# Second products of two MLPs and a gated network as seven accumulated block products

## The reference

```python
# twice, D_FF = 4096
h = rms_norm(x, ln_mlp_pre[l])
x = x + rms_norm(jnp.square(jax.nn.relu(h @ mlp_w1[l])) @ mlp_w2[l], ln_mlp_post[l])
# once, D_FF_2 = 2816
x = x + (jax.nn.silu(h @ w1) * (h @ w3)) @ w2
```

## Time and profile before

| | us |
|---|---|
| median of 3 runs | 2972.57 |
| lowest and highest | 2966.53, 2977.65 |
| the profiled execution | 2970.6 |
| its span, first to last instruction | 2968.8 |
| mean granted TensorE clock | 0.986 of full |
| first MLP, from hT's second half to the last second product | 539.46 to 744.11 |
| second MLP | 1259.31 to 1464.0 |
| gated network | 1609.1 to 1830.1 |

### The profile page before, as it was taken

One profiled execution on the slowest core, in us unless ns is written; L12 is line 12 of the kernel. 1 busy time (PEld: TensorE's weight loads), 2 busy tenths in 40 slices (PEclk: granted clock), 3 DMA queues, 4 the chain that ended last, 5 costly groups with the idle time before them and its releaser, 6 DMA issues.

```text
span 2968.8 us, 37497 instructions
## 1 busy us (share of the span) xinstructions
PE 2845.2 (96%) x16514; PEld 2101.4 (71%) x16514; DVE 824.2 (28%) x1461; ACT 336.2 (11%) x687; POOL 91.0 (3%) x130
## 2 busy tenths in 40 slices
PE   7999998999999999899999999989999999999998
PEld 6689775676678867577676777557776776776775
DVE  2554112434255311233444453230001001001001
ACT  1220211000222111100032000210000000000000
POOL 0011200000001110000000000000000000000000
PEclk9999999999999999999999999989999999999999
DMA  5231342444333243244342433339999999999995
GB/s 228 92 142 72 135 154 80 163 170 171 107 135 114 74 154 141 100 156 163 131 154 114 164 134 120 136 125 381 378 362 362 385 352 363 386 356 370 372 386 233
DMA packets 59193, 617.18 MB, mean 208 GB/s; under 512 B 6800, under 2 KB 7056, under 8 KB 8976
## 3 DMA queue, kind: packets, MB, share of 16 engines
q1 hardware_dynamic: 56880, 603.27, 52.8%
q0 software_dynamic: 2144, 11.45, 1.0%
HBM read 613.64 MB, written 1.05 MB: 207 GB/s over the span
## 4 chain that ended last, share of the span: by engine, by line
PE 88%; DVE 5%; DMA 4%; ACT 1%; issue 1%; SPq 0%; DVEq 0%; ACTq 0%
PE ps L680 14%; PE ps L1403 14%; PE ps L1119 8%; PE ps L1126 8%; PE ps L1010 8%; PE ps L1413 7%; PE ps L1423 6%; PE ps L990 4%; PE ps L1443 3%; PE ps L1022 2%; PE ps L661 2%; PE ps L721 2%; DMA slabA<-in_ev_ffn_w 1%; PE ps L1101 1%; PE ps L1284 1%
## 5 line engine op out<-in xcount | busy, mean ns | idle before, releaser
L1403 PEld LDWEIGHTS ps<-work,slabA 128*128 128x128 f32 x3584 | 406.0, 192 | 45.2 <-issue 45.2
L1403 PE MATMUL ps<-work,slabA 128*128 128x128 f32 x3584 | 416.7, 277 | 0.9 <-issue 0.9
L1126 PE MATMUL ps<-slabB,work 128*128 128x512 f32 x688 | 301.9, 592 | 0.0
L1010 PE MATMUL ps<-hT,slabA 128*128 128x256 f32 x1024 | 232.3, 380 | 1.1 <-ACT work L1635 1.1
L1126 PEld LDWEIGHTS ps<-slabB,work 128*128 128x128 f32 x688 | 127.7, 190 | 145.4 <-issue 145.4
L680 PE MATMUL ps<-hT,slabA 128*128 128x256 f32 x992 | 219.5, 381 | 1.3 <-DMA slabA<-in_ev_w_in 0.7
L1010 PEld LDWEIGHTS ps<-hT,slabA 128*128 128x128 f32 x1024 | 192.2, 190 | 28.3 <-ACT work L1635 1.9
L680 PEld LDWEIGHTS ps<-hT,slabA 128*128 128x128 f32 x992 | 187.9, 191 | 28.0 <-issue 1.4
L1413 PE MATMUL ps<-fbT,work 128*64 128x256 f32 x1792 | 205.7, 382 | 1.8 <-DMA fbT<-in_od_exp_w 1.8
L1423 PE MATMUL ps<-slabB,work 128*128 128x512 f32 x448 | 202.0, 593 | 0.0
L1413 PEld LDWEIGHTS ps<-fbT,work 128*64 128x64 f32 x1792 | 123.6, 137 | 85.5 <-issue 26.3
(11 more groups left out here) (373 smaller groups left out, 2757.3 us busy)
## 6 DMA issues: line engine op xcount, KB each, us to landing
slabA<-in_od_exp_w SPq DMA_DIRECT2D x56, 2048.0 KB, 9.6
fbT<-in_od_exp_w SPq DMA_DIRECT2D x56, 2048.0 KB, 9.9
slabB<-in_od_exp_w SPq DMA_DIRECT2D x56, 1024.0 KB, 8.4
fbT<-in_od_exp_w SPq DMA_DIRECT2D x56, 1024.0 KB, 10.7
slabA<-in_w_in SPq DMA_DIRECT2D x24, 2048.0 KB, 7.8
slabA<-in_mlp_w SPq DMA_DIRECT2D x32, 1024.0 KB, 6.8
slabB<-in_mlp_w SPq DMA_DIRECT2D x32, 1024.0 KB, 4.8
slabA<-in_ev_ffn_w SPq DMA_DIRECT2D x11, 2048.0 KB, 10.6
```

Of the source, the lines that this page charges most:

```text
L1010: last = mm(ps[:, b, 0:T], side["gates"][:, k, c % 4 * P:(c % 4 + 1) * P], hT[:, k, :], start=(k == 0), stop=(k == KD - 1))
L1126: last = mm(ps[:, 4 + 2 * t + half, :], he[:, j, t * P:(t + 1) * P], w2[:, j, half * 512:(half + 1) * 512], start=(i == 0 and j == 0), sto ...
L1403: last = mm(ps[:, 0, (2 * w + j) * P:(2 * w + j + 1) * P], v[:, k, j * P:(j + 1) * P], xs[:, k, :], start=(k == 0), stop=(k == KD - 1))
```

## The change

The second product of a step is also made as seven block products, of 128 hidden columns x 128 tokens with 512 columns each. Each of the seven has a PSUM bank of its own, 1 to 7, in which it accumulates over all steps but the last two; then they are combined once, in PSUM (`first_tokens`, `second_tokens`), and the last two steps are added to the result in the old form. For this VectorE forms four sums of slabB (`down_sums_of`) and four of the hidden block (`hidden_sums_of`) in each step. The block products of the first product have only bank 0 left: they are made in groups of four and three, ScalarE copies each group to SBUF, and the next group waits for that copy. TensorE therefore takes groups of the first product and parts of the second in turn. `combine` reads the copies and needs one operation less. The weight sums have two buffers instead of three, and three semaphores of other stages (`fox_ln`, `gla_cum`, `gla_exps`) are replaced by ones that exist already, with the same order.

The new parts and the loops, cut (the code that they replace is printed above; `up_sums` forms the sums of slabA as `sums` did, `gate_of` and `hidden` call `combine` and add the Silu's product or the square, `plain` is a plain step; in the gated network the stage begins with the token sums, `up_sums(1, 0)`, `plain(0)`, `down_sums_of(0)`, `hidden_sums_of(0)`, `up_sums(1, 1)`):

```diff
+        def up_bank(i, w, part, steps):
+            return 2 * w + part if i == steps - 1 else 0
...
-                ringA.load(sp, [((lambda s: s[:, 0:w13.shape[1]]), w13)], ("hidden_psum", 2) if i < plain_steps(gated) else ("up_products", 1 + gated))
+                ringA.load(sp, [((lambda s: s[:, 0:w13.shape[1]]), w13)], ("hidden_psum", 2) if i < plain_steps(gated) else ("up_products", 2 * (1 + gated)))
...
+                    factors = ((a11, b11), (a12, b21), (sa[:, 0], sb_[:, 0]), (sa[:, 1], sb_[:, 1]), (sa[:, 2], sb_[:, 2]), (sa[:, 3], b22), (a22, sb_[:, 3]))
+                    bank = up_bank(i, w, part, steps)
+                    if bank > 1:
+                        pe.wait_ge(sem("sums_ready"), due("pe", "sums_ready"))
+                    elif (i, w, part) != (begun, 0, 0):
+                        pe.wait_ge(sem("products_out"), due("pe", "products_out"))
+                    for c, (lhs, rhs) in enumerate(factors[4 * part:4 * part + 4]):
+                        if c == 2 and part == 0:
+                            pe.wait_ge(sem("sums_ready"), due("pe", "sums_ready"))
+                        for k in range(4):
+                            last = mm(ps[:, bank, c * P:(c + 1) * P], lhs[:, k, :], rhs[:, k, :], start=(k == 0), stop=(k == 3))
+                    last.then_inc(sem("up_products"), up("up_products"))
+                def down_products(i, w2, c0, c1):
+                    he, hs, ws = hidden_of_step(i), hidden_sums(i), down_sums(i)
+                    if c0 == 0:
+                        pe.wait_ge(sem("sums_ready"), due("pe", "sums_ready", 2))
+                    for b, lhs, rhs in ((4, he[:, 2, :], w2[:, 1, 0:512]), (5, hs[:, 3, :], w2[:, 1, 512:D]), (6, he[:, 3, :], ws[:, 3, :]), (7, hs[:, 0, :], ws[:, 0, :]),
+                                        (2, hs[:, 1, :], ws[:, 1, :]), (3, hs[:, 2, :], ws[:, 2, :]), (1, he[:, 0, :], w2[:, 0, 0:512]))[c0:c1]:
+                        if i == 0 and b == 2:
+                            pe.wait_ge(sem("hidden_ready"), due("pe", "hidden_ready", 2 * begun))
+                        last = mm(ps[:, b, :], lhs, rhs, start=(i == 0), stop=(i == steps - 3), skip_group_check=True)
+                    if b == 1:
+                        last.then_inc(sem("slabB_used"), up("slabB_used"))
...
                 for i in range(begun, steps - 1):
                     s = ringA.take(pe)
+                    up_products(i, 0, s, 0)
+                    w2 = down_slab()
                     if gated:
-                        w2 = take_hidden(i - 1)
-                    products(i, s)
-                    if not gated:
-                        w2 = take_hidden(i - 1)
-                    rows_both(i - 1, w2)
+                        down_products(i - 1, w2, 0, 2)
+                        up_products(i, 0, s, 1)
+                        down_products(i - 1, w2, 2, 4)
+                        up_products(i, 1, s, 0)
+                        down_products(i - 1, w2, 4, 6)
+                        up_products(i, 1, s, 1)
+                        down_products(i - 1, w2, 6, 7)
+                    else:
+                        down_products(i - 1, w2, 0, 3)
+                        up_products(i, 0, s, 1)
+                        down_products(i - 1, w2, 3, 7)
+                begun_at.append(slabs_at + (count_of("slabB_used").posted,))
                 i = steps - 1
                 s = ringA.take(pe)
-                w2s_ = [take_hidden(i - 1)] if gated else []
-                products(i, s)
+                for w in range(1 + gated):
+                    for part in range(2):
+                        up_products(i, w, s, part)
+                w2_ = [down_slab()]
                 if not gated:
-                    w2s_.append(take_hidden(i - 1))
-                rows_of(i - 1, w2s_[0], 0)
-                w2s_.append(take_hidden(i))
-                rows_of(i, w2s_[1], 0).then_inc(sem(edges), up(edges))
-                rows_of(i - 1, w2s_[0], 1).then_inc(sem("slabB_used"), up("slabB_used"))
-                rows_of(i, w2s_[1], 1).then_inc(sem(edges), up(edges))
+                    pe.wait_ge(sem("sums_ready"), due("pe", "sums_ready"))
+                pe.wait_ge(sem("hidden_ready"), due("pe", "hidden_ready"))
+                rows_of(i - 1, w2_[0], 0)
+                w2_.append(down_slab())
+                pe.wait_ge(sem("products_out"), due("pe", "products_out", 2 * (1 + gated)))
+                pe.wait_ge(sem("hidden_ready"), due("pe", "hidden_ready"))
+                rows_of(i, w2_[1], 0).then_inc(sem(edges), up(edges))
+                if not gated:
+                    pe.wait_ge(sem("sums_ready"), due("pe", "sums_ready"))
+                rows_of(i - 1, w2_[0], 1).then_inc(sem("slabB_used"), up("slabB_used"))
...
+                accumulated = begun_at[drained.pop(0)][2]
+                for i in range(plain_steps(gated), steps):
+                    for w in range(1 + gated):
+                        p = products_in(i, w, gated)
+                        for part, c in enumerate((slice(0, 4), slice(4, 7))):
+                            act.wait_ge(sem("up_products"), due("act", "up_products"))
+                            nc.scalar.activation(p[:, c, :], ps[:, up_bank(i, w, part, steps), 0:(c.stop - c.start) * P].rearrange("p (c t) -> p c t", t=P), ACT.Copy).then_inc(sem("products_out"), up("products_out"))
+                            act.wait_ge(sem("products_out"), at("products_out"))
+                            if w and part == 0:
+                                act.wait_ge(sem("gate_sums"), due("act", "gate_sums"))
+                                a1 = U(2 + i % 2, size=512)
+                                nc.scalar.activation(a1, a1, ACT.Silu).then_inc(sem("hidden_act"), up("hidden_act"))
+                                act.wait_ge(sem("hidden_act"), at("hidden_act"))
+                    if i == steps - 2:
+                        act.wait_ge(sem("slabB_used"), accumulated)
+                        nc.scalar.activation(U(12, size=512), ps[:, 1, :], ACT.Copy).then_inc(sem("products_out"), up("products_out"))
+                        act.wait_ge(sem("products_out"), at("products_out"))
...
+                def down_sums_of(i):
+                    w2, ws = loaded(ringB, slab2 + i).rearrange("p (j h n) -> p j h n", j=2, h=2), down_sums(i)
+                    sub(ws[:, 0, :], w2[:, 0, 1, :], w2[:, 0, 0, :])
+                    sub(ws[:, 1, :], w2[:, 1, 1, :], ws[:, 0, :])
+                    sub(ws[:, 2, :], w2[:, 1, 1, :], w2[:, 0, 1, :])
+                    v.tensor_tensor(ws[:, 3, :], w2[:, 1, 0, :], ws[:, 1, :], ALU.subtract).then_inc(sem("sums_ready"), up("sums_ready"))
+                    dve.wait_ge(sem("sums_ready"), at("sums_ready"))
+                def hidden_sums_of(i):
+                    he, hs = hidden_of_step(i), hidden_sums(i)
+                    add(hs[:, 0, :], he[:, 1, :], he[:, 3, :])
+                    sub(hs[:, 1, :], hs[:, 0, :], he[:, 0, :])
+                    sub(hs[:, 2, :], he[:, 0, :], he[:, 1, :])
+                    v.tensor_tensor(hs[:, 3, :], he[:, 2, :], hs[:, 1, :], ALU.subtract).then_inc(sem("sums_ready"), up("sums_ready"))
+                    dve.wait_ge(sem("sums_ready"), at("sums_ready"))
...
+                def combine(i, w, d, done="dve_order"):
+                    p = products_in(i, w, gated)
+                    both = U(2, off=512, size=2 * P).rearrange("p (c t) -> p c t", c=2)
+                    dve.wait_ge(sem("products_out"), due("dve", "products_out", 2))
+                    add(d[:, 0:4:3, :], p[:, 1:4:2, :], p[:, 0:1, :].broadcast_to([P, 2, P]))
+                    add(both, p[:, 2:5:2, :], d[:, 3:4, :].broadcast_to([P, 2, P]))
+                    add(d[:, 1:3, :], both, p[:, 5:7, :])
+                    v.tensor_tensor(d[:, 3, :], both[:, 1, :], p[:, 2, :], ALU.add).then_inc(sem(done), up(done))
                     dve.wait_ge(sem(done), at(done))
...
+                def first_tokens():
+                    dve.wait_ge(sem("slabB_used"), accumulated)
+                    dve.wait_ge(sem("products_out"), due("dve", "products_out"))
+                    add(ps[:, 4, :], ps[:, 4, :], sum_1)
+                    add(sum_2, ps[:, 2, :], sum_1)
+                    add(sum_3, ps[:, 7, :], sum_2)
+                    v.tensor_tensor(ps[:, 5, :], ps[:, 5, :], sum_3, ALU.add).then_inc(sem("sums_ready"), up("sums_ready"))
+                    dve.wait_ge(sem("sums_ready"), at("sums_ready"))
+                def second_tokens():
+                    add(sum_3, ps[:, 3, :], sum_2)
+                    add(ps[:, 6, :], ps[:, 6, :], sum_3)
+                    v.tensor_tensor(ps[:, 7, :], ps[:, 7, :], sum_3, ALU.add).then_inc(sem("sums_ready"), up("sums_ready"))
+                    dve.wait_ge(sem("sums_ready"), at("sums_ready"))
...
+                else:
+                    down_sums_of(0)
+                    plain(0)
+                    hidden_sums_of(0)
```

(55 more changed lines are left out.)

117 lines of the change are left out of this document (66 added, 51 removed).

## The result

| | before | after |
|---|---|---|
| median of the runs beside each other | 2975.11 (4) | 2953.18 (4) |
| lowest and highest | 2966.53, 2978.99 | 2952.70, 2953.55 |
| the profiled execution, its span | 2970.6, 2968.8 | 2953.55, 2951.8 |
| first MLP, hT's second half to the last second product | 204.83 | 202.00 |
| second MLP | 204.83 | 201.74 |

What follows compares the result with a forecast made beforehand. TensorE, busy 96% of the span, was taken as the bound. Gains of 3 us (MLPs) and 15 (gated network) off 2970.6 gave 2952.6; the median, 2 us above, 2954.5. Own range 2946 to 2962, whole range 2936 to 2969.

Steps and rivals of the forecast that it cites:

- the slab chain: MLP step: slabA's landing, VectorE's sums and combination, signal to TensorE; 17.3 us from step start, taking back nearly all of 0.86.
- MLP, 3 us forecast: Both MLPs together gain 3 us: 0.09 x 26, plus step 0 (2 x 0.86), less about 1.
- the "about 1" charged for late landings: MLPs: about 1 us lost where a slab landing near 9 us meets a step without a stall to spare.
- The restart: MLP: extra time of TensorE's first passes after a stall, 0.07 us (0.08 in the chain's sum).
- the stalls: MLP: TensorE's waits before second products; two consecutive ones sum to 1.4 us, 0.70 on average per step.
- the term with most leverage: MLP gain through landing or chain: 0.5 us there is 0.25 per step, 6.5 us in all.
- Gated network, 15 forecast: Gated steps 18.9 us, 1.8 less, times 8 = 14.3; first step gains 1.3, last gives back 0.5; total 15.
- The first step's new stall: Gated network's first step: a new stall of 2.0 us for two sets of sums, replacing two shorter ones.
- A handoff: Bank 0, TensorE to ScalarE's copy and back: 1.02 or 0.91 us, mostly covered by second products.
- The first (no chain): Rival: the slab chain does not bind, MLPs keep their 24 us and the gated network 15; 2933 us, chance 0.13.
- The second: Rival: the gated gain is lost to the one bank, handoffs taking 1.9 us; 2966 us, chance 0.17.
- The third: Rival: regular stalls bring the granted clock down, 50 us over some 28 stalls; 3005 us, chance 0.08.

Runs made afterwards that it cites:

- e7: The changed kernel with one of slabB's four sums formed twice in every MLP step, 0.73 us more on VectorE; 2966.66 us.
- e1: The changed kernel, but in the MLPs VectorE forms the sums of slabB before those of slabA; 2942.81 us.
- e2: The changed kernel, but in the MLPs SP issues slabA of step i+1 before slabB of step i, VectorE's order kept; 2934.62 us.
- e5: The changed kernel with slabB's sums first, but in the MLPs all seven second products come after both groups of block products, so handoffs are uncovered; 2966.04 us.
- e3: The changed kernel with slabB's four sums formed twice in every MLP step, 2.9 us more on the chain; 3031.32 us.

## Why the prediction was right, and where its terms were off

2954.5 was forecast and 2953.18 measured, by the mechanism named: the MLP's gain mostly given back to the slab chain, the gated network's kept.

**MLP, 3 us forecast, 5.9 measured.** 2.8 and 3.1 came off the two stages. The prediction counts from the first block product in the timeline, which stands 0.17 us ahead of the chain's 566.10; counted so, the chain was 17.2 us long in the step shown against 17.3, VectorE's part 9.53 against 9.5 and the landing 7.5 against 7.7. The step became 12.98 against 13.03, which is 1.3 of the 2.9 us missing over 26 steps. Most of the rest is the "about 1" charged for late landings, which did not come: in after the 26 first sums run 7.4 to 7.9 us after their steps' starts, where before had four at 8.7 to 9.0. The restart was undersized, 0.07 against 0.23 (six passes 2.81, elsewhere 2.58), and the stalls oversized, 0.70 a step against 0.48 in the two shown (0.64 and 0.32); the two misses nearly cancel, 0.77 against 0.71 a step. They cancel because the sum takes the restart off the stalls as well as adding it to the step. That 0.5 us on the chain is worth 0.25 per step was the term with most leverage; e7 (0.40 for 0.73) bears it out, and e1 and e2 the 12.26 below it.

**Gated network, 15 forecast, 15.3 measured.** The step took 18.86 against 18.9, 0.35 over its work where 0.4 was charged, at the step's end and in the restart, where they were put. Over half of what a step gained was the wait, as the prediction's 1.8 against 0.86 of work implies but does not say. The first step's new stall was 1.8 against 2.0.

**The bank.** A handoff was priced at 0.91 to 1.02 if bare; e5 has 1.04. The copies of ScalarE take 0.49 for 384 columns (0.49 was taken):

```profile
1670.96 0.49 ACT L1675 ACTIVATE work<-ps 128x384 f32<-128x384 f32 x1 [3.14 <-PE ps L1138]
```

By the 186 ns and 0.833 ns a column of the Trainium skill, "ScalarE: Activation LUTs", What ACT_TABLE_LOAD costs, an estimate is 0.51; the trace is 0.02 below it.

**The sum** came out within 1.3 us by luck: two misses offset. The MLPs gave 3 us more than forecast. The three stages together gave 21.2 us, but the spans differ by 17.0, so 4.2 us were lost outside the edit, for which the forecast had no term. Between the MLPs, 3.4 us of it, the same 2511 instructions of TensorE take 487.43 us busy before and, after, at a clock lower by 0.01:

```profile
741.92:1260.31 518.39, 490.94 (x2511) 385.69 (x2510) 171.07 (x260) 93.94 (x181) 43.52 (x60) 0.98 0.32 118
```

Over the whole span both profiles read 0.986, so the clock does not account for all of the 4.2; the rest stays open. The median of before had also moved up, to 2975.11.

**The rivals.** The first (no chain) needed landings or an order that the kernel lacked; e1 and e2 made it true, and their 193.3 against after's 202.0 is its price, 17.1 us for both MLPs. The second fell with e1, and by the gated step's 0.11. The third did not come in the change, where stalls are at most 1.8 us, and came in e3 at 3.7 and more. The Trainium skill, "TensorE: Matmul & The Clock Gate", A second HAM failure mode, warns, from a bf16 kernel, of cycling through PSUM banks with micro-idles. This kernel goes through eight banks in a step, with a stall in each step of its first MLP, and shows 1.00.

## What to carry to other kernels

When a faster scheme adds work to the engine that feeds TensorE, follow that work in program order back to the transfer it stands behind, and from there to what the transfer itself is queued behind: here either of two reorderings, with not one operation fewer, raised the gain of the MLPs from 5.9 to 23 us. Where a chain spans one step and part of the next, and TensorE stalls on it, stalls of consecutive steps share it: here 0.73 us on the chain cost 0.40 per step. Keep apart what fewer operations save and what a new order saves; in the gated network the order was more than half. Judge an edit worth a few us by the lengths of its own stages, when the rest of the program varies by more.

## What the runs showed of the hardware

Stalls of 0.2 to 0.8 us in each step of 13 us, of 1.1 to 1.2 in every other one (after), and of 0.5 to 1.2 in each (e7) left the granted clock at 1.00, as did a single one of 1.8. Stalls of 3.7 us and more, about every 30.6 us (e3), were each followed by a clock of 0.50 to 0.64 over the next 4 us; the one shown, of 4.1, cost 1.9 on top of itself. Between these the outcome varied: behind the same wait of 2.65 us elsewhere in the kernel the clock was lower in 12 cases of 20. In stretches that no edit touched, such differences moved the time by up to 10 us between kernels.

A handoff from TensorE through PSUM and ScalarE back to TensorE took 1.04 us, only 0.84 of which is listed as a wait. A transfer of 1 MB landed 4.8 us after its issue (e2), and 6.9 when it was issued right behind another of 1 MB (after).
